# Scaled one-hot tables of the gates stage: from GpSimd to ScalarE, in eight products per block

## What is computed

```python
s = jnp.einsum('thpc,hpkc->thpk', q, sub_keys)          # 8 heads, two halves, 128 keys each
top_s, top_i = lax.top_k(s, PEER_TOPK)                  # 16 of 128 in each half
best_s, best_c = lax.top_k(cand, PEER_TOPK)             # 16 of the 256 sums
ids = i1 * N_KEYS + i2                                  # expert = (i1, i2)
g = jax.nn.softmax(best_s, axis=-1)
act = jax.nn.gelu(jnp.einsum('td,thkd->thk', xb, u_tab[ids]))
return jnp.einsum('thk,thkd->td', g * act, v_tab[ids])
```

## Time and profile before

| what | value |
|---|---|
| median of 3 runs | 2824.27 us (2818.85 to 2828.52) |
| profiled execution | 2821.09 us |
| its span in the trace | 2819.3 us |
| TensorE busy | 2739.9 us (97%) |
| VectorE busy | 2276.7 us (81%) |
| GpSimd busy | 1498.6 us (53%) |
| ScalarE busy | 1032.8 us (37%) |
| one table load of ScalarE (ACT_TABLE_LOAD L905) | 1283 ns |

### The profile page before, as it was taken

One profiled execution on the slowest core, in us unless ns is written; L12 is line 12 of the kernel. 1 busy time (PEld: TensorE's weight loads), 2 busy tenths in 40 slices (PEclk: granted clock), 3 DMA queues, 4 the chain that ended last, 5 costly groups with the idle time before them and its releaser, 6 DMA issues.

```text
span 2819.3 us, 33411 instructions
## 1 busy us (share of the span) xinstructions
PE 2739.9 (97%) x11792; PEld 2095.5 (74%) x11792; DVE 2276.7 (81%) x3813; ACT 1032.8 (37%) x1372; POOL 1498.6 (53%) x1202
## 2 busy tenths in 40 slices
PE   8989899999999999999999999999999999999998
PEld 3444445887778888888778888888888888888886
DVE  1985524788998888898688898988989889898986
ACT  4443524112355666665323223232222323223233
POOL 3892200220023666665377767777777777777630
PEclk9999999999999999999999999999999999999999
DMA  5110101112647999999999898898989889898983
GB/s 195 45 45 1 60 15 45 60 43 93 217 143 240 327 333 344 339 339 356 385 342 329 300 318 318 302 325 303 330 293 321 310 310 326 301 325 300 339 301 139
DMA packets 254838, 687.75 MB, mean 244 GB/s; under 512 B 32080, under 2 KB 97744, under 8 KB 249168
## 3 DMA queue, kind: packets, MB, share of 16 engines
q0 software_dynamic: 104448, 335.81, 34.1%
q1 hardware_dynamic: 84432, 316.27, 31.3%
q10 hardware_dynamic: 65792, 33.56, 4.1%
HBM read 614.22 MB, written 71.30 MB: 243 GB/s over the span
## 4 chain that ended last, share of the span: by engine, by line
PE 71%; DVE 11%; DMA 8%; POOL 4%; DVEq 3%; issue 2%; ACT 1%; ACTq 0%; POOLq 0%; SPq 0%
PE ps L1832 25%; PE ps L1824 24%; PE ps L1745 6%; DMA vring<-in_u_tab,idsA 6%; PE ps L1797 5%; PE ps L1619 4%; DVE ps L1025 2%; POOL hnT L526 2%; DVE vring L1409 1%; DVE lx L1240 1%; PE ps L1783 1%; PE ps L1526 1%; DVE marks L1352 1%; POOL vring L584 1%; PE ps L1732 1%
## 5 line engine op out<-in xcount | busy, mean ns | idle before, releaser
L596 POOL DMA_INDIRECT vring<-in_v_tab,idsA x512 | 556.4, 1087 | 302.2 <-DVE ps L1392 165.4
L1392 DVE SCALAR_TENSOR_TENSOR ps<-vring,hsel,ps 128x1024 f32<-128x1024 f32 x508 | 652.7, 1285 | 26.2 <-DMA vring<-in_v_tab,idsA 9.7
L571 POOL DMA_INDIRECT hsel<-hidden,idsE x384 | 408.1, 1063 | 124.6 <-issue 104.6
L1832 PE MATMUL ps<-vh,wl 128*128 128x512 f32 x1024 | 406.6, 397 | 0.0
L1832 PE MATMUL ps<-vh,wh 128*128 128x512 f32 x1024 | 402.8, 393 | 3.2 <-DVE acc L1469 3.2
L1824 PE MATMUL ps<-xh,ul 128*128 128x512 f32 x1024 | 404.1, 395 | 0.0
L1824 PE MATMUL ps<-xh,uh 128*128 128x512 f32 x1024 | 403.3, 394 | 0.7 <-ACT hlast L858 0.7
L1832 PE MATMUL ps<-vl,wh 128*128 128x512 f32 x1024 | 403.0, 394 | 0.0
L1824 PE MATMUL ps<-xl,uh 128*128 128x512 f32 x1024 | 402.1, 393 | 0.0
L954 ACT CAST vh<-v_raw 128x1024 fp32r<-128x1024 f32 x128 | 134.0, 1047 | 591.4 <-PE ps L1832 584.5
L1797 PE MATMUL ps<-hx,xh 128*128 128x512 f32 x768 | 312.7, 407 | 29.6 <-DVE lx L1240 25.8
(11 more groups left out here) (197 smaller groups left out, 4701.2 us busy)
## 6 DMA issues: line engine op xcount, KB each, us to landing
xraw<-in_uX SPq DMA_DIRECT2D x128, 512.0 KB, 6.0
u_raw<-in_uT SPq DMA_DIRECT2D x128, 512.0 KB, 6.2
v_raw<-in_v_tab SPq DMA_DIRECT2D x128, 512.0 KB, 7.1
gates<-gbuf ACTq DMA_DIRECT2D x16, 2048.0 KB, 24.1
gt<-gates SPq DMA_DIRECT2D x32, 1024.0 KB, 9.0
hidden<-hst SPq DMA_DIRECT2D x93, 256.0 KB, 8.2
wbuf<-in_w_in SPq DMA_DIRECT2D x19, 512.0 KB, 3.6
wqbuf<-in_w_q SPq DMA_DIRECT2D x16, 512.0 KB, 3.6
```

The costliest lines, as they stand in the source:

```text
L571: nc.gpsimd.indirect_dma_start(out=hsel[:, n, k:k + 1], out_offset=None, in_=hidden_items, in_offset=bass.IndirectOffsetOnAxis(ap=idsE[:, ...
L596: nc.gpsimd.indirect_dma_start(out=vring[q % VS][:, :], out_offset=None, in_=v_rows, in_offset=bass.IndirectOffsetOnAxis(ap=idsA[:, n, k:k ...
L1392: nc.vector.scalar_tensor_tensor(out=bank2(6), in0=vring[slot][:, :], scalar=w, in1=bank2(6), op0=ALU.mult, op1=ALU.add).then_inc(cb_done, 1)
L1832: last = mm(ps[:, 2 + k % 4, :], w[:, c, tt * P:(tt + 1) * P], v[:, c, dh * 512:(dh + 1) * 512], start=c == 0 and w is wh and v is vh, sto ...
```

## The change

GpSimd's `scale_hot` and its calls are gone. ScalarE makes the scaled table right behind the plain one of the same block, in eight instructions, one per token: 128 elements of `marks`, read at a step of two, times a scalar per partition, one column of `selG`. The last of the eight raises `hot_scaled`; the start credit of this semaphore moves to ScalarE. Who waits for `hot_scaled` (VectorE's `mark`, TensorE's `hot_block`, SyncE once at the end of the stage) is as before.

```diff
-            def scale_hot(n):
-                i, b = divmod(n, BLOCKS)
-                pool.wait_ge(hot_eq, n + 1)
-                pool.wait_ge(gp_ready, (n + 1) * HQ)
-                gate = selG[:, i, b * HOT:(b + 1) * HOT].rearrange("p (c e) -> p c e", e=2)
-                nc.gpsimd.tensor_tensor(hot[:, b % ROWS, 1, :, :].rearrange("p (c e) k -> p c e k", e=2),
-                                        marks[:, b % RAW, 1, :, :, :].rearrange("p c k e -> p c e k"),
-                                        gate.unsqueeze(3).to_broadcast([P, HOT // 2, 2, NKEY]),
-                                        ALU.mult).then_inc(hot_scaled, 1)
-
...
-            pool.sem_inc(hot_scaled, RAW)
             for Q in range(QUARTERS):
-                for n in range(HT * BLOCKS):
-                    if hot_quarter(n) - 1 == Q:
-                        scale_hot(n)
                 for k in range(P):
                     if quarter_of_dot(k) - 2 == Q:
                         gather_dot(k)
...
                 nc.scalar.copy(hot[:, b % ROWS, 0, :, :].rearrange("p (c e) k -> p c e k", e=2),
                                marks[:, b % RAW, 0, :, :, :].rearrange("p c k e -> p c e k")).then_inc(hot_plain, 1)
+                for t in range(HOT):
+                    last = nc.scalar.mul(hot[:, b % ROWS, 1, t, :], marks[:, b % RAW, 1, t // 2, :, t % 2],
+                                         selG[:, i, b * HOT + t:b * HOT + t + 1])
+                last.then_inc(hot_scaled, 1)
...
             act.sem_inc(hot_plain, RAW)
+            act.sem_inc(hot_scaled, RAW)
```

## The result

| what | before | after |
|---|---|---|
| median of the runs | 2822.33 us (2818.85 to 2828.52, 5 runs) | 2804.22 us (2800.59 to 2804.72, 5 runs) |
| profiled execution | 2821.09 us | 2804.72 us |
| its span | 2819.3 us | 2802.9 us |
| VectorE busy | 2276.7 us | 2230.0 us |

The medians differ by 18.1 us. The ratio is 0.9929, with a 95% interval of 0.9918 to 0.9939, which is 20 us (17 to 23) of 2822. The forecast was 2813.8 with a range from 2806: the sign was right, the gain 1.7 to 1.9 times the 10.5 us forecast, and the time just outside the range. It is near rival (c), "everything goes" (2806.8), but not by its terms: ScalarE's cost, which (c) left out, is there, and the other gains are larger.

What follows compares the result with a forecast made beforehand. TensorE was taken as the bound, losing time in the gates stage to waits for VectorE's `lx`. Stage -12, tail -1.5 and ScalarE +3 made -10.5 us: 2813.8 us for the median, range 2806 to 2836.

Steps and rivals of the forecast that it cites:

- rival (c): Whole gain: all 13 us of the stage, half the tail, nothing on ScalarE; -17.5, 2806.8 us; chance 0.08.
- The mechanism: Gates stage: GpSimd's product lengthens VectorE's `marks` and `lx`; removing it gives VectorE back at least 14.6 us.
- the tail: After 1320 us: VectorE enters a little further ahead, transfers set its pace; gain 1.5 of 6.3 us.
- The stage's term: Gates stage: TensorE's waits for `lx` and one low clock, 13 us to be had, 12 taken as gain.
- GpSimd's own queue: Gathers of `u` rows: issued at most one product (2 us) earlier, mostly not at all; counted as nothing.
- ScalarE's term: Gates stage: loss of 3 us in all, 2.8 of it TensorE's wait for `hst` at 1275.27.
- Its budget: ScalarE in the gates stage: work with the products sums to 14.6 of 16.05 us, so it fits.
- a trio: Gates stage: TensorE's recurring pattern of two blocks in three quarters, 16.05 us, 31.5 of them in the stage.
- The row of four `vv`: Four similar ScalarE products in the trace, 1.14 us together; basis for taking 0.28 us per new product.
- rival (b): Gates stage: ScalarE becomes the bound, from 0.37 us per product; +18 in the middle, 2842 us; chance 0.22.
- faster: Whole kernel: a median under 2815.8 us, 8.5 us being about what a measurement can tell; chance 0.44.
- (a): Transfers take over, VectorE waits longer for `u` rows, only the early stretch pays; -3.5, 2820.8 us; chance 0.20.

Runs made afterwards that it cites:

- e1_read_product: Changed kernel, with GpSimd again making two products per block from constants into an unread spare tile: 2823.87 us, ratio 1.0011 to the kernel before.
- e2b_fills_no_drain: Changed kernel, with two GpSimd fills per block into a spare tile, reading nothing, no drain between: 2808.79 us, ratio 0.9959 to the kernel before.
- the repetition: The changed kernel run once more, unaltered, on the same chip as three follow-up runs: 2802.15 us, ratio 0.9929 to the kernel before.
- experiment 3: Changed kernel with three or six more ScalarE products per block into an unread spare tile: 2839.83 and 2898.92 us.
- e4_three_more: Changed kernel with three more ScalarE products per block, behind the eight, into an unread spare tile: 2839.83 us, ratio 1.0061 to the kernel before.
- experiment 4: Changed kernel with the last `xraw` load started earlier (2801.10 us), ScalarE's products held behind evictions where both meet (2801.42), or both (2800.88).
- e2_write_only: Changed kernel, with four GpSimd fills per block into a spare tile and a drain between two pairs: 2925.92 us, ratio 1.0372 to the kernel before.

## Why the prediction was right or wrong

**The mechanism** was right in the stage: e1_read_product takes the gain back with ScalarE's part left in place, and e2b_fills_no_drain keeps 11.6 us of it with GpSimd nearly as busy as before (266 of 500 us against 276).

**The step that failed** is the tail: "freed of GpSimd it enters the tail a little further ahead, but the transfers set its pace. I take 1.5 of the 6.3 us". It was 6.5 in the profiled execution and 3.8 in the repetition. The transfers did not set the pace of its first eleven quarters: with lead these took 46.0 us instead of 54.3, a gain of 8.3. They do set the last quarter, which gave back 1.8 us in the profiled execution and 4.4 in the repetition. Two windows over the same last twelve quarters, of before and of after:

```profile
1317.60:1377.20 59.60, 53.27 (x221) 41.50 (x220) 36.95 (x53) 17.45 (x22) 20.24 (x14) 0.97 1.00 374
```

```profile
1308.00:1361.00 53.00, 50.40 (x221) 40.68 (x219) 29.56 (x41) 15.97 (x20) 14.04 (x11) 1.00 1.01 380
```

The idle time fell from 6.33 to 2.60 us, and the busy time by 2.9: behind the longest wait of before (4.54 us, ending at 1361.96) products followed each other every 0.43 us instead of 0.235 until 1365.9:

```profile
1361.96 0.50 PE L1797 MATMUL ps<-hx,xh 128*128 128x512 f32 x1 [4.54 <-DVE lx L1240]
...
1363.33 0.63 PE L1797 MATMUL ps<-lx,xh 128*128 128x512 f32 x1
1363.76 0.63 PE L1797 MATMUL ps<-hx,xl 128*128 128x512 f32 x1
```

The window over that stretch shows the granted clock at 0.51, the lower of its two levels (1.2 of 2.4 GHz), and 10 products in 3.40 us:

```profile
1362.50:1365.90 3.40, 3.40 (x10) 2.63 (x9) 1.08 (x1) 0.00 (x0) 0.21 (x1) 0.51 1.00 406
```

This low clock is gone with the wait. "A little further ahead" was 12.5 us instead of 2.2. The root is a term that the prediction put at nothing without a reason: "The other instructions of VectorE with two operands in SBUF come on top; I don't count them." It counted 14.6 us and left "at least" open; VectorE's busy time fell by 46.7 us. What TensorE doesn't need of that becomes lead, and with it the late `u` rows no longer reach TensorE before the last quarter.

**The stage's term** was mis-sized too, by 3.4 us in the profiled execution and 3.8 in the repetition, where the tail's was off by 5.0 and 2.3: 12 forecast, 15.4 measured (15.8 from quarter 24 on, and 15.8 in the repetition). "So 13 us are to be had in the stage, and no more" counted the listed waits and one dip of the clock; the restart of each of 12 waits was missing, 0.25 us each, and so 16 us were to be had, not 13.

**GpSimd's own queue**, counted at nothing, was worth up to 5 to 8 us by e2b_fills_no_drain. This isn't a further term: it is part of the same gains, mostly of the last quarter.

**ScalarE's term** was right in place and size: forecast 2.8 at the place of the earlier trace rows and 3 in all, measured 2.78 there (before: 0.34), 2.5 in the quarters' table. Its budget, with 1.45 us over in a trio, was too wide (experiment 3). The lines of ScalarE and of TensorE at that place:

```profile
1261.05 2.44 ACT L878 ACTIVATE hot<-marks,selG 128x128 f32<-128x128 bf16 x8
1263.51 1.28 ACT L895 ACT_TABLE_LOAD   x1
1264.81 0.22 ACT L895 ACTIVATE hsel<-hsel 128x16 f32<-128x16 f32 x1
1264.93 1.54 ACT L844 COPY hst<-ps 128x512 f32<-128x512 f32 x3
...
1265.55 0.50 PE L1788 MATMUL ps<-hx,xh 128*128 128x512 f32 x1 [2.78 <-ACT hst L844]
```

Eight products take 2.44 us with the last one's end of about 0.39, so (2.44 - 0.39)/7 = 0.29 us from start to start; forecast 0.28, with 0.26 to 0.30 named. The row of four `vv` was the right neighbour. The estimate from the Trainium skill (ScalarE: Activation LUTs, Rules for kernel authors), 0.41 us, fits the duration of one (0.394) and not the pace; at 0.41 the rival (b) would have come, as e4_three_more shows (11 products at 0.29 fill ScalarE like eight at 0.40, and cost 36 us; (b) had been priced at 2842 us, and this run took 2839.8).

**The chances.** The forecast stood on the right mechanism, yet faster had only 0.44, because (a) and (b) held 0.42. (b) was a fair rival with 0.34 us as its point. (a) was wrong in the stage and in eleven quarters of the tail, and true for its last quarter, where experiment 4 found transfers setting the end.

In sum, per step and against -10.5: the stage -15.4, the tail -6.5 and ScalarE +2.5 make -19.4; 3.2 us ahead of it went the other way in the profiled execution, and the medians differ by 18.1.

## What to carry to other kernels

When a change gives an engine that others wait for more time back than they lose, carry the surplus on as lead and ask which later waits it covers; don't stop at the waits of the stage itself. Count all instructions that get shorter, not the two largest groups. Then ask what the lead can't cover: a transfer that is issued late for reasons of its own. Price a wait of TensorE at its listed length plus the restart, and plus the low clock behind a long one. And before work goes to an engine with room, work out from the pace, not from durations, at which count it becomes the bound, and take off the idle time that the order of its list leaves unusable: here the estimate from experiment 3 is about nine products per block, and eight were moved.

## What the runs showed of the hardware

A drain on GpSimd waited for its indirect transfers in flight. In 790 to 1400 of e2_write_only GpSimd stood still 49 times for 256.8 us ahead of fills, 5.2 us each and up to 9.3; without the drain it was 44.3 us in 22 times. In all 50 blocks that had gathers in flight, the fill behind the drain started 0.15 to 0.23 us after the last of these gathers had landed. In the 14 blocks ahead of the first gather it started within 0.12 us. One of the 50, with VectorE's instruction that the same landing released:

```profile
1013.76 1.22 DVE L1417 SCALAR_TENSOR_TENSOR vring<-vring,ps 128x1024 f32<-128x1024 f32 x1 [4.19 <-DMA vring<-in_u_tab,idsA]
```

```profile
1013.88 0.99 POOL L561 MEMSET spare<- 128x512 bf16 x2 [6.29 <-issue]
```

An instruction of VectorE with one input in SBUF was lengthened as well, beside reads and beside fills. The lines are of before, of after and of e2b_fills_no_drain, each in 800 to 1300:

```profile
L1286 DVE TENSOR_SCALAR bdig<-bpos 128x128 uint32<-128x128 uint32 x25 | 10.7, 493 | 0.0
```

```profile
L1277 DVE TENSOR_SCALAR bdig<-bpos 128x128 uint32<-128x128 uint32 x25 | 4.1, 246 | 0.0
```

```profile
L1292 DVE TENSOR_SCALAR bdig<-bpos 128x128 uint32<-128x128 uint32 x25 | 8.3, 583 | 0.0
```

Busy time is 4.1 us alone, 10.7 with the product on GpSimd and 8.3 with fills. Few of the 25 make the difference: 3 beside a product took 2.53 us each, 4 beside fills 2.38 to 2.45, the others 0.22 in the mean, and some beside the start of a gather up to 0.42. Each long one ended some 0.1 us after GpSimd's instructions, as here in e2b_fills_no_drain:

```profile
1095.96 2.78 DVE L1292 TENSOR_SCALAR bdig<-bpos 128x128 uint32<-128x128 uint32 x4
```

```profile
1096.47 1.86 POOL L559 MEMSET spare<- 128x1024 uint8 x2
```

So here writing alone disturbs, unlike with `lx` and `marks`. The Trainium skill (SBUF — State Buffer, Who interferes with whom) has a rule that fits: an operation of this kind can use both ports of VectorE for its one input and contends with GpSimd then. The prediction left it uncounted, 6.6 us in this stretch.
